# Seven block products in place of eight in the first part of the output projection

## The reference

```python
xn = rms_norm(x, norm_mix[l])
... = jnp.split(xn @ w_in[l], split_at, axis=-1)
y_mla = mla_mixer(...)      # 8 heads, 512 wide
y_dil = dilated_mixer(...)  # 12 heads, 768 wide
y_ml = mlstm_mixer(...)     # 4 heads, 768 wide
x = x + jnp.concatenate([y_mla, y_dil, y_ml], axis=-1) @ w_out[l]
x = x + hier_moe(rms_norm(x, norm_ffn[l]), ...)
```

## Time and profile before

| | us |
|---|---|
| median of 3 runs | 1902.62 (1899.58 to 1903.28) |
| the profiled execution's own time | 1901.18 |
| its span, as the profile has it | 1899.4 |
| TensorE matmul busy | 1856.9 (98%) |
| VectorE busy | 625.1 (33%) |
| ScalarE busy | 312.2 (16%) |
| oa stage with its steps, layer 2 (1268.5 to 1369.0) | 100.5 |
| gather and eight expert pairs of layer 1 (490.0 to 948.8) | 458.8 |

### The profile page before, as it was taken

The page is one execution under the profiler, slowest core; times in us unless marked ns, Lnnn a source line. Parts: engine busy times, 40 slices in busy tenths (PEclk is TensorE's granted clock), DMA queues, the critical chain, the costliest instruction groups (busy, mean ns, idle before and its releaser), DMA issues.

```text
span 1899.4 us, 26494 instructions
## 1 busy us (share of the span) xinstructions
PE 1856.9 (98%) x11558; PEld 1402.2 (74%) x11558; DVE 625.1 (33%) x1361; ACT 312.2 (16%) x845; POOL 7.4 (0%) x15
## 2 busy tenths in 40 slices
PE   7999999999999999999899999999999999999998
PEld 6788887788866666656597888877878656666655
DVE  3477664222211211121235675632231121221112
ACT  2122222111211111011021131331120111111010
POOL 0000000000000000000000000000000000000000
PEclk9999999999999999999999999999999999999999
DMA  9342345153699999999794243351647999999995
GB/s 349 140 172 105 161 178 203 69 213 141 270 425 427 427 428 426 428 426 428 304 376 159 113 178 131 136 227 45 266 160 296 426 426 428 426 428 426 428 428 248
DMA packets 40551, 544.68 MB, mean 287 GB/s; under 512 B 4744, under 2 KB 4872, under 8 KB 7792
## 3 DMA queue, kind: packets, MB, share of 16 engines
q1 hardware_dynamic: 38448, 531.46, 67.8%
q0 software_dynamic: 1728, 11.42, 1.5%
q10 hardware_dynamic: 256, 0.04, 0.0%
HBM read 538.69 MB, written 4.22 MB: 286 GB/s over the span
## 4 chain that ended last, share of the span: by engine, by line
PE 97%; issue 1%; DVE 1%; DMA 1%; SPq 0%; ACT 0%; DVEq 0%
PE ps L712 94%; PE ps L766 1%; DMA ring<-in_w_lat 1%; PE ps L1125 1%; PE ps L782 0%; PE ps L774 0%; PE ps L1043 0%; PE ps L1167 0%; PE ps L871 0%; DVE v_mla L1782 0%; DVE scr L1751 0%; PE ps L923 0%; DVE prob L1842 0%; DVE scr L1754 0%; DVE scr L1753 0%
## 5 line engine op out<-in xcount | busy, mean ns | idle before, releaser
L712 PE MATMUL ps<-ring,scr 128*64 128x256 f32 (+2 forms) x3520 | 555.8, 425 | 7.1 <-issue 7.1
L712 PEld LDWEIGHTS ps<-ring,scr 128*64 128x64 f32 (+1 forms) x3520 | 316.4, 138 | 202.3 <-issue 113.0
L712 PE MATMUL ps<-ring,XN 128*128 128x256 f32 (+2 forms) x1184 | 244.2, 363 | 12.8 <-DMA ring<-in_w_lat 12.8
L712 PEld LDWEIGHTS ps<-ring,XN 128*128 128x128 f32 x1184 | 212.4, 191 | 33.4 <-issue 14.0
L712 PE MATMUL ps<-ring,X 128*128 128x256 f32 x896 | 200.6, 379 | 0.0
L712 PEld LDWEIGHTS ps<-ring,X 128*128 128x128 f32 x896 | 169.6, 190 | 22.7
L712 PE MATMUL ps<-XN,ring 128*128 128x256 f32 x768 | 170.4, 381 | 0.9 <-DVE prob L1311 0.9
L712 PEld LDWEIGHTS ps<-XN,ring 128*128 128x128 f32 x768 | 144.7, 190 | 26.6 <-issue 7.7
L712 PE MATMUL ps<-BIAS,scr 128*64 128x256 f32 (+1 forms) x608 | 155.9, 414 | 5.0 <-issue 5.0
L712 PE MATMUL ps<-PR,scr 128*64 128x256 f32 (+2 forms) x576 | 160.0, 434 | 0.7 <-DVE scr L1835 0.7
L1824 DVE TENSOR_TENSOR v_mla<-scr,ps 128x256 f32<-128x256 f32 x32 | 13.5, 421 | 424.1 <-PE ps L712 424.1
(11 more groups left out here) (250 smaller groups left out, 1253.2 us busy)
## 6 DMA issues: line engine op xcount, KB each, us to landing
ring<-in_moe_w_up SPq DMA_DIRECT2D x44, 2048.0 KB, 22.7
ring<-in_moe_w_down SPq DMA_DIRECT2D x44, 2048.0 KB, 26.8
ring<-in_moe_w_gate SPq DMA_DIRECT2D x42, 2048.0 KB, 24.5
ring<-in_w_main SPq DMA_DIRECT2D x36, 2048.0 KB, 9.0
ring<-in_w_out_a SPq DMA_DIRECT2D x10, 2048.0 KB, 8.4
PR<-in_moe_w_down SPq DMA_DIRECT2D x10, 2048.0 KB, 24.1
XN<-in_moe_w_gate SPq DMA_DIRECT2D x10, 2048.0 KB, 28.1
BIAS<-in_moe_w_up SPq DMA_DIRECT2D x10, 2048.0 KB, 23.4
```

The source lines that it names most:

```text
L712: return pe.matmul(o, lhsT, rhs, start=start, stop=stop, skip_group_check=True)
```

## The change

In the oa stage the eight chunks are taken as four pairs, u = 0 to 3, and the tokens as two halves of 128. Each pair is made with seven block products in place of eight. A product (`product_a`) is 2 x 5 `mm` calls: five tiles of one half of the attention channels, two halves of 128 output channels, and 128 tokens. The ten tiles are dealt into two halves of five (`A_ROWS`), and the host lays the weights out to match, so `w_out_a` now comes as eight loads A0 to A7, one for each chunk, of 1.25 MB. VectorE makes four weight sums for a pair (`a_sums`, 128 x 1280 each), four activation sums for a layer (`ya_sums`), and adds the products to X in pieces of 256 elements (`evict_a`). The steps keep their numbers: count 4u + 0, 1, 2, 3 is now reached after p6, w, p5 and c12 of pair u (`STEP_AFTER`). SyncE issues the router's weights behind A4 as before, and A5 to A7 behind them.

```diff
+N_APAIR = N_OUT // 2
+HA = K_A // 2
+HALF_A = HA * CH
+A_ROWS = (0, 1, 4, 5, 6, 2, 3, 7, 8, 9)
...
-    for j in range(N_OUT):
-        b.once(f"oa{j}", j % 2)
+    for u in range(N_APAIR):
+        for name in PRODUCTS:
+            b.once(f"a{name}_{u}", (u + (name in ("p6", "w", "c21"))) % 2)
...
+LAST_READER.update({f"A{j}": f"a{('c21', 'c12')[j % 2]}_{j // 2}" for j in range(N_OUT)})
...
+                for j in range(N_OUT):
+                    if j == 5:
+                        sp.wait_ge(*copied(f"do{H_D // 2 - 1}", l))
+                        sp.dma_start(w_rt.rearrange("p k c -> p (k c)"), a["w_router"][l]).then_inc(rw_in, 16)
+                    load(f"A{j}", l, a["w_out_a"][l, j], width=2 * HALF_A)
...
+            def product_a(name, u, l):
+                one, two = 2 * u, 2 * u + 1
+                w, y, half, first = {
+                    "p1": (a_part(one, 0), (0, 0), 0, True), "p6": (a_part(two, 2), 1, 0, True),
+                    "c11": (a_part(one, 1), (0, 1), 0, False), "w": (a_part(two, 0), 2, 0, False),
+                    "p5": (a_part(one, 2), 0, 1, True), "c21": (a_part(one, 1), (1, 1), 0, False),
+                    "c12": (a_part(two, 1), 3, 1, False)}[name]
+                if name == "p1":
+                    pe.wait_ge(*loaded(f"A{one}", l))
+                    pe.wait_ge(*loaded(f"A{two}", l))
+                if name in ("p6", "w", "p5", "c21"):
+                    pe.wait_ge(*after({"p6": "a2", "w": "a3", "p5": "a1", "c21": "a4"}[name], l, u))
+                if u == 0 and name in ("p6", "w"):
+                    pe.wait_ge(*after("ya_sums", l, ("p6", "w").index(name)))
+                name = f"a{name}_{u}"
+                pe.wait_ge(*freed(name, l))
+                for q in range(2):
+                    for i in range(HA):
+                        rhs = ya_sum[:, y, i, :] if type(y) is int else ya_tile(*y, i)
+                        last = mm(bank(name)[:, half * CH + q * P:half * CH + (q + 1) * P], w[:, i * CH + q * P:i * CH + (q + 1) * P], rhs,
+                                  first and q == 0 and i == 0, i == HA - 1)
+                last.then_inc(*made(name))
...  TensorE's loop
-                for j in range(N_OUT):
-                    for q in range(2):
-                        project_out("a", j, q, l)
-                        if 2 * j + q in MLSTM_AT:
+                for u in range(N_APAIR):
+                    for name in PRODUCTS:
+                        product_a(name, u, l)
+                        if name not in STEP_AFTER:
+                            continue
+                        at = 4 * u + STEP_AFTER[name]
+                        if at in MLSTM_AT:
...
-                        if 2 * j + q == MIX_AT:
+                        if at == MIX_AT:
                             mixed(l)
...  VectorE
+                def a_sums(n, u):
+                    one, two = 2 * u, 2 * u + 1
+                    t1, t2 = a_part(one, 2), a_part(two, 2)
+                    if n == 1:
+                        for j in (one, two):
+                            dve.wait_ge(*loaded(f"A{j}", l))
+                        dve.tensor_tensor(t1, a_part(two, 0), a_part(one, 0), ALU.subtract).then_inc(*signal("a1"))
...
+                    else:
+                        dve.wait_ge(*ready(f"ac11_{u}", l))
+                        dve.wait_ge(*after("a2", l, u))
+                        dve.tensor_tensor(a_part(one, 1), a_part(one, 1), t2, ALU.subtract).then_inc(*signal("a4"))
+                def ya_sums():
+                    dve.wait_ge(*ready(f"m{N_SEQ - 1}", l))
+                    dve.wait_ge(*copied(f"ao{H_A // 2 - 1}", l))
+                    dve.wait_ge(*copied(f"do{H_D // 2 - 1}", l))
...
+                def evict_a(name, u):
+                    dve.wait_ge(*ready(f"a{name}_{u}", l))
+                    behind = {"p6": "p1", "w": "p1", "p5": "w", "c21": "p1", "c12": "p6"}
+                    if name in behind:
+                        dve.wait_ge(*copied(f"a{behind[name]}_{u}", l))
...
+                    if name == "p1":
+                        dve.tensor_tensor(two, two, o.unsqueeze(2).to_broadcast([P, 2, 2, P]), ALU.add)
...
+                    dve.tensor_tensor(x, x, o, ALU.add).then_inc(*read(f"a{name}_{u}"))
...
+                for n in (1, 2, 3):
+                    a_sums(n, 0)
+                ya_sums()
                 dve.wait_ge(rw_in, (l + 1) * 16)
...
-                        if q == 1:
-                            add_out(f"oa{j}", j)
+                        evict_a(name, u)
+                        if name == "c11":
+                            a_sums(4, u)
+                        if name in ("c11", "w", "p5") and u + 1 < N_APAIR:
+                            a_sums(("c11", "w", "p5").index(name) + 1, u + 1)
+                        if name not in STEP_AFTER:
+                            continue
+                        at = 4 * u + STEP_AFTER[name]
...
-                        if 2 * j + q == MIX_AT:
+                        if at == MIX_AT:
                             mix(l)
```

More of the change, by code:

```diff
@@ L877, in project_out @@
+            def project_out(j, q, l):
+                name, n_k = f"ob{j}", KT - K_A
                 if q == 0:
                     pe.wait_ge(*freed(name, l))
[L879 to L884, removed]
+                for k in range(n_k):
+                    at = j * n_k + k
+                    if q == 0 and (k == 0 or at % TILES == 0):
+                        pe.wait_ge(*loaded(f"B{at // TILES}", l))
+                    w = slot(f"B{at // TILES}")[:, at % TILES * CH:(at % TILES + 1) * CH]
+                    last = mm(bank(name)[:, q * S:(q + 1) * S], w[:, q * P:(q + 1) * P], y_t(K_A + k), k == 0, k == n_k - 1)
@@ new lines, in ya_sums @@
+                def ya_sums():
+                    dve.wait_ge(*ready(f"m{N_SEQ - 1}", l))
+                    dve.wait_ge(*copied(f"ao{H_A // 2 - 1}", l))
+                    dve.wait_ge(*copied(f"do{H_D // 2 - 1}", l))
+                    at = (slice(0, 2), slice(2, HA))
+                    for i in range(2):
+                        own.did(dve.tensor_tensor(ya_sum[:, 0, at[i], :], ya_pieces(1, 0)[i], ya_pieces(1, 1)[i], ALU.add))
+                    own.wait()
+                    for i in range(2):
+                        ins = dve.tensor_tensor(ya_sum[:, 1, at[i], :], ya_sum[:, 0, at[i], :], ya_pieces(0, 0)[i], ALU.subtract)
+                    ins.then_inc(*signal("ya_sums"))
+                    for i in range(2):
+                        own.did(dve.tensor_tensor(ya_sum[:, 2, at[i], :], ya_pieces(0, 0)[i], ya_pieces(1, 0)[i], ALU.subtract))
+                    dve.wait_ge(*after("ya_sums", l, 0))
+                    own.wait()
+                    for i in range(2):
+                        ins = dve.tensor_tensor(ya_sum[:, 3, at[i], :], ya_pieces(0, 1)[i], ya_sum[:, 1, at[i], :], ALU.subtract)
+                    ins.then_inc(*signal("ya_sums"))
@@ new lines, in evict_a @@
+                def evict_a(name, u):
[3 more added lines that the diff above has]
+                        dve.wait_ge(*copied(f"a{behind[name]}_{u}", l))
+                    o = bank(f"a{name}_{u}")[:, CH * (name in ("p5", "c12")):][:, 0:CH].rearrange("p (q s) -> p q s", q=2)
+                    one, two = (X[:, 4 * u + 2 * j:4 * u + 2 * j + 2, :].rearrange("p k (t s) -> p k t s", t=2) for j in range(2))
+                    if name == "p1":
+                        dve.tensor_tensor(two, two, o.unsqueeze(2).to_broadcast([P, 2, 2, P]), ALU.add)
+                    x = {"p1": one[:, :, 1, :], "p6": two[:, :, 0, :], "p5": two[:, :, 1, :], "c11": one[:, :, 0, :],
+                         "w": two[:, :, 1, :], "c12": two[:, :, 0, :], "c21": one[:, :, 1, :]}[name]
+                    dve.tensor_tensor(x, x, o, ALU.add).then_inc(*read(f"a{name}_{u}"))
@@ L1711, in _ @@
                                 both_ways(h - 1)
-                        if 2 * j + q == MIX_AT:
+                        if at == MIX_AT:
                             mix(l)
                 for j in range(N_OUT):
-                    dve.wait_ge(*copied(f"oa{j}", l))
+                    for n in ("c21", "p5", "c12"):
+                        dve.wait_ge(*copied(f"a{n}_{j // 2}", l))
                     add_out(f"ob{j}", j)
```

51 lines of the change are left out of this document (30 added, 21 removed).

## The result

The changed kernel takes 1914.99 us (median of 4 runs, 1913.49 to 1915.61), the kernel before 1902.93 us beside it (1899.58 to 1903.28). The ratio is 1.0063, with a 95% interval of 1.0050 to 1.0075: slower by 12 us, where 1898.7 us was predicted and 1905.2 us was the upper end of the range. The profiled execution took 1914.54 us with a span of 1912.7 us.

The account below looks back on a forecast made before the run. The oa stage was taken as bound by TensorE: 2 x (6.5 - 3.7) = 5.6 us gained, less 1.7 us for one clock fall, is 3.9 us off 1901.2, so 1897.3, or 1898.7 us as median; range 1891.4 to 1905.2 us.

Parts of the forecast that it names:

- The matmuls: oa stage: 560 instructions of 128 columns at 0.1117 us replace 320 of 256, saving 6.5 us in a layer.
- VectorE: oa stage: its weight sums and additions, 38 us in a layer, stay hidden behind TensorE and cost zero.
- its slack of 0.3 us: Pair 2 of the oa stage: p5 is emptied at 8.4 us and c12 asks at 8.7 us, the tightest place.
- The wait for the mix: Last pair of the oa stage: TensorE idles before `mixed` until VectorE's mix is done, 3.7 us in a layer.
- The clock: Behind the wait for the mix: TensorE's granted clock falls in one of the two layers, costing 1.7 us.
- the rival with two falls: Behind the mix: the clock falls in both layers, costing 3.4 us, for 1900.4 us; chance 0.27.
- and the end moves with it: Experts' phase: its stream of loads starts earlier by what the oa stage gains, and the kernel's end moves equally.
- every slot is then full: Start of the experts: loads go out until 478.6 us, the next at 505.6 us when the first product frees its slot.
- nothing here is on the path: Loads: same 10 MB in a layer, A0 to A7, B0 to B2 and the experts' tiles delay nothing.
- narrow matmuls above 0.1168 us: oa stage: weight loads set the pace at 0.1197 us an instruction, 70.7 us a layer, for 1907.6 us; chance 0.10.
- two that the trace cleared: Slower shares of 0.05 each: VectorE late at the banks (1905.2 us, chance 0.14) and narrow matmuls (1907.6 us, chance 0.10).

Follow-up runs that it names:

- before with 392 waits: Kernel before with never-executed waits added to TensorE's program, 392 in the first layer's sweep block and 120 in the second's: 1903.16 us.
- the early mix with 24 waits: Changed kernel with the mix's nine VectorE instructions ahead of w's eviction, and 24 never-executed waits in the first layer's sweep block: 1891.65 us.
- its wait filled: Changed kernel with 24 never-executed waits in the first layer's sweep block and 13 dummy products ahead of the mix's transposes in each layer: 1898.94 us.
- without the filling: Changed kernel with 24 never-executed waits added to TensorE's program in the first layer's sweep block: 1904.38 us.
- the two pairs with another mix: Changed kernel, mix ahead of p5's eviction or its instructions ahead of w's, each without and with 24 never-executed waits: 1906.85 and 1895.53 us; 1903.37 and 1891.65 us.
- after_mixearly: Changed kernel with the mix's nine VectorE instructions ahead of w's eviction in the last pair, code left in place: 1903.37 us.
- its old rotation: Changed kernel with the experts' tiles put in the slots in the order of the kernel before: 1913.91 us.
- the two with an earlier mix: Changed kernel with the mix ahead of p5's eviction, or its nine instructions ahead of w's, code not moved: 1906.85 and 1903.37 us.
- before with 472 waits: Kernel before with 472 never-executed waits added to TensorE's program in each layer's sweep block: 1916.79 us.
- after_mixearly_oldslots_shift24: Changed kernel with the mix's instructions ahead of w's eviction, 24 never-executed waits, and the experts' slots in the order of before: 1888.81 us.

## Why the prediction was wrong

**The matmuls: right.** 0.1118 us measured for 0.1117. The saving can be read where layer 2 has no clock fall in either kernel: from the first product of the stage to the first of the experts, before with 392 waits, then the early mix with 24 waits (the timeline first, then the chain):

```profile
1278.18 8.90 PE L712 MATMUL ps<-PR,ring 128*128 128x256 f32 x40
```

```profile
1437.84 20.94 PE ps L712 x192
```

```profile
1275.00 2.50 PE L739 MATMUL ps<-PR,ring 128*128 128x128 f32 x20
```

```profile
1428.66 20.94 PE ps L739 x192
```

159.66 - 153.66 = 6.0 us, and 0.3 us of it is still given to the mix: 6.3 for the 6.5 us predicted. With the mix where the change put it and its wait filled, the same stretch is 156.7 us: 2.9 us less than before, for the 2.8 us (6.5 - 3.7) that the prediction gave a layer without a clock fall.

**VectorE: right.** It shows no wait at a bank beyond the expected ones, not even in pair 2 with its slack of 0.3 us; TensorE's list of waits has only the mix and what before had. Its sums took 1.48 us for 1.49.

**The wait for the mix: right.** 3.4 us for 3.7, in the place and by the order that was named.

**The clock: right in the price of a fall, wrong in their number.** One fall of 1.7 us was taken; both layers fell, which the rival with two falls had at 3.4 us and a chance of 0.27. A fall costs 1.65 us as predicted, but each here came with a second one in the routing: four falls, 6.6 us by the traces of layer 2, 5.4 us by the medians with and without the filling. The rule of the Trainium skill (TensorE: Matmul & The Clock Gate, What's actually happening), by which an idle stretch drops the clock, would have had both falls, and the trace agrees with it (0.57 of full clock behind the wait); the prediction did not price the second ones.

**The step that failed: "and the end moves with it".** Its first half held: the experts' phase starts when the work ahead of it is done and keeps its length (457.8 to 460.6 us from the first gather matmul to the last product, in both layers of all sixteen traces). But from "every slot is then full" the prediction went to the end of the kernel as if nothing behind the experts could change. From the end of layer 1's products to layer 2's first oa product before takes 328.3 us and the changed kernel 337.3; from the end of layer 2's products to the end of the span, 12.3 and 16.3 us. It counted the 560 matmuls only by their time. It asked neither what 492 instructions more do to the code behind them, which costs 10.6 us (1915.0 - 1904.4; 11.3 and 11.7 us in the two pairs with another mix), nor what another number of tiles does to the rotation of the slots, of which it said "nothing here is on the path". The page of before showed queue q8 with 96 packets, and I did not ask it anything.

With these figures the sum is 1902.9 - 2 x 6.3 + 2 x 3.4 = 1897.1 us. The kernel with the wait filled, which should take that, has 1898.9 us; the 1.8 us between are no more than it loses behind the first branch, where it waits 3.2 us and before 1.0. The other steps are the measured differences themselves: the clock falls 5.4 us (1904.4), the place of the code 10.6 us (1915.0). Of the 16.3 us between forecast and result the place of the code is the largest part, then the 3.7 us of falls that the forecast did not count.

**The rivals.** The named way to get slower, narrow matmuls above 0.1168 us, didn't happen. The rival with both falls was right about them and put the time at 1900.4 us, 14.6 us too low. No rival had the mechanism that decided, and 0.10 of the chance of 0.12 for slower lay on two that the trace cleared.

## What to carry to other kernels

When a change alters how many instructions an engine's program has ahead of a branch, the code behind the branch shifts against its 16 KB blocks; compare the waits on "issue" right behind each branch before any part of the time difference is put down to the edit itself, and move the code with a few instructions in a block that is never entered. A wait of a few microseconds on TensorE costs more than its length where the clock falls behind it, so put what TensorE will ask for ahead of the eviction that it just released. Two kernels whose times are equal may hide a gain and a fault of the same size, as after_mixearly and before do here.

## What the hardware showed that was not expected

- A branch whose target is at the end of a block of code cost TensorE 6.4 to 9.3 us of idle time within the kernel and 2.2 to 2.5 us at its end, where the DMA queues are nearly idle, at 4 GB/s in the changed kernel (five traces: the changed kernel, its old rotation, the two with an earlier mix, and before with 472 waits). In the table's kernels two fetches in a row start 5.0 to 6.8 us apart at the first branch, and so they do where the queues are nearly idle (940.2 and 946.1 us in the kernel before, at 39 GB/s); at the kernel's end the target's packet and the next are 3.0 to 3.5 us apart in those five. What sets these intervals stays open.
- Executions of one kernel differ along with their mean clock: the five of after_mixearly_oldslots_shift24 run from 1886.38 us at 0.999 to 1892.65 us at 0.996. So a difference of a few microseconds between kernels should not be read from a single one.
- 26 dummy matmuls in an idle stretch of TensorE, in each layer, made the kernel 5.4 us faster (1904.4 to 1898.9 us, eleven runs each).
